# Retention stage of a two-block transformer forward: one weight split moved ahead of a wait, half splits moved into the last head, and a statistics matmul moved into the output projection

## The reference, cut to what matters

```python
def _odd_mixer(x, pos, w_in, w_out):
    p = x @ w_in                                  # 1024 -> 6144
    q, k, v, g = jnp.split(p, [qk, 2 * qk, 2 * qk + RET_MIX], axis=-1)
    q = _rope(q.reshape(B, T, RET_HEADS, RET_QK_DIM), pos)
    k = _rope(k.reshape(B, T, RET_HEADS, RET_QK_DIM), pos) * (RET_QK_DIM ** -0.5)
    ...
    # retention: (q k^T * decay) v, in chunks with a carried state
    ...
    o = of * lax.rsqrt(jnp.mean(jnp.square(of), axis=-1, keepdims=True) + EPS)
    y = o.transpose(0, 2, 1, 3).reshape(B, T, RET_MIX)
    return (jax.nn.silu(g) * y) @ w_out           # 2048 -> 1024
```

## Time and profile before

| what | value |
|---|---|
| median of three runs | 3351.13 us |
| the profiled execution's own time | 3334.76 us |
| its span in the profile | 3332.9 us |
| TensorE busy, share of the span | 2965.2 us, 89% |
| DVE, ACT, POOL busy | 1449.0, 896.7, 625.8 us |
| mean granted TensorE clock | 0.935 of full speed |
| retention, first head's start to the layer norm's end | about 734 to 1235 us of the span |
| the two expert stages | about 1795 to 2335 and 2745 to 3290 us |

### The profile page before, as it was taken

How to read it: one execution, slowest core, us unless ns; L and a number is a source line. 1 busy time by engine, 2 the same in 40 slices (tenths; PEclk the granted TensorE clock), 3 DMA queues, 4 the chain that set the end, 5 groups by cost and what they waited for, 6 DMA issues and landing times.

```text
span 3332.9 us, 42752 instructions
## 1 busy us (share of the span) xinstructions
PE 2965.2 (89%) x17700; PEld 2311.2 (69%) x17700; DVE 1449.0 (43%) x2553; ACT 896.7 (27%) x1600; POOL 625.8 (19%) x540
## 2 busy tenths in 40 slices
PE   7889999999999899999997998888598897988883
PEld 6658999998888678888786555555476675555552
DVE  4553422343444443233544443332697735533334
ACT  3442422332222334232322111111235621211111
POOL 1202201130111122011101432221200002522221
PEclk9987999999999999999998999999799998999996
DMA  4011232222221123323224999999421019999995
GB/s 133 14 63 44 71 100 85 96 73 81 80 65 66 51 76 101 101 89 101 76 76 181 374 409 409 409 408 390 156 74 59 27 36 371 406 409 410 409 409 219
DMA packets 271813, 600.30 MB, mean 180 GB/s; under 512 B 32375, under 2 KB 177202, under 8 KB 255226
## 3 DMA queue, kind: packets, MB, share of 16 engines
q1 hardware_dynamic: 247408, 569.47, 45.6%
q0 software_dynamic: 23968, 27.93, 2.6%
q10 hardware_dynamic: 234, 0.06, 0.0%
HBM read 607.75 MB, written 39.89 MB: 194 GB/s over the span
## 4 chain that ended last, share of the span: by engine, by line
PE 82%; DVE 8%; issue 4%; DMA 3%; ACT 2%; POOL 1%; SPq 1%; DVEq 0%; POOLq 0%; ACTq 0%
PE ps L101 76%; PE ps L104 6%; DVE sb_arena L126 1%; DVE sb_arena L118 1%; POOL sb_arena L118 1%; DVE sb_tmpA L118 1%; SPq L144 1%; DMA sb_ring<-in_exp_w_dram 1%; DMA sb_hx<-in_exp_w_dram 1%; DVE sb_tmpA L122 1%; DVE sb_tmpA L126 1%; DVE sb_hs L118 0%; DMA sb_arena<-x_rows,sb_smallu 0%; ACT sb_hs L112 0%; DVE sb_small L1539 0%
## 5 line engine op out<-in xcount | busy, mean ns | idle before, releaser
L101 PE MATMUL ps<-sb_hs,sb_ws 128*128 128x264 f32 (+1 forms) x6384 | 1121.1, 338 | 40.5 <-DVE sb_ws L118 27.0
L101 PEld LDWEIGHTS ps<-sb_hs,sb_ws 128*128 128x128 f32 x6384 | 985.4, 193 | 173.0 <-DVE sb_ws L118 28.1
L118 DVE TENSOR_TENSOR sb_ws<-sb_ring,sb_ws 128x1024 fp32r<-128x1024 f32 x279 | 367.4, 1320 | 431.4 <-ACT sb_ws L112 430.9
L101 PE MATMUL ps<-sb_arena 128*64 128x256 f32 (+16 forms) x2068 | 385.8, 436 | 52.9 <-issue 31.2
L112 ACT CAST sb_ws<-sb_ring 128x1024 fp32r<-128x1024 f32 x279 | 290.5, 1045 | 374.0 <-PE ps L101 356.1
L101 PE MATMUL ps<-sb_br,sb_ws 128*128 128x264 f32 (+1 forms) x2304 | 366.5, 321 | 0.0
L101 PE MATMUL ps<-sb_ring,sb_arena 128*64 128x256 f32 (+2 forms) x2314 | 319.7, 432 | 52.1 <-issue 50.9
L101 PEld LDWEIGHTS ps<-sb_br,sb_ws 128*128 128x128 f32 x2304 | 332.3, 188 | 33.7
L101 PEld LDWEIGHTS ps<-sb_arena 128*64 128x64 f32 (+6 forms) x2068 | 227.8, 167 | 156.5 <-issue 85.5
L104 PEld LDWEIGHTS ps<-sb_cst,sb_arena 128*128 128x128 f32 (+3 forms) x1032 | 155.1, 204 | 201.3 <-DVE sb_arena L118 82.2
L101 PEld LDWEIGHTS ps<-sb_ring,sb_arena 128*64 128x64 f32 (+1 forms) x2314 | 193.4, 147 | 145.6 <-issue 85.1
(11 more groups left out here) (182 smaller groups left out, 2233.6 us busy)
## 6 DMA issues: line engine op xcount, KB each, us to landing
sb_ring<-in_exp_w_dram SPq DMA_DIRECT2D x160, 1024.0 KB, 21.2
sb_hx<-in_exp_w_dram SPq DMA_DIRECT2D x128, 1024.0 KB, 21.4
sb_arena<-in_exp_w_dram SPq DMA_DIRECT2D x96, 1024.0 KB, 21.4
sb_ring<-in_mlp_w_dram SPq DMA_DIRECT2D x64, 1024.0 KB, 5.3
sb_ring<-in_od_w_in_dram SPq DMA_DIRECT2D x24, 1024.0 KB, 5.2
sb_ring<-in_conv_w_in_dram SPq DMA_DIRECT2D x12, 1024.0 KB, 5.0
sb_ring<-in_attn_w_in_dram SPq DMA_DIRECT2D x10, 1024.0 KB, 5.9
sb_ring<-in_od_w_out_dram SPq DMA_DIRECT2D x8, 1024.0 KB, 5.1
```

The source lines that it names most:

```text
L101: return self.e.matmul(o, l, r, start=start, stop=stop, skip_group_check=True)
L118: return self.e.tensor_tensor(o, a, b, op)
```

## The change

On ACT and DVE the split beside v0 (that is v2's) is now called before the wait for y0 to y3, and in the loop over v and g the first tile calls none. On ACT the upper halves of `YR` tiles 0 to 7 are made in head 3 after the copies of v, before the copies of the weighting's outputs; on DVE the lower halves follow the scores of head 3. Tiles 8 to 11 (head 2's) are split between the squares and the square root, 12 to 15 after it. On TensorE the ones matmul of head 3 is no longer ahead of the output projection but in its first pair, at step k == 4.

```diff
-        def dense(e, stage, cols, K, rhs, T, units, pair=True):
+        def dense(e, stage, cols, K, rhs, T, units, pair=True, between=None):
...
                         for k in range(kn + 2):
+                            if k == 4 and between is not None:
+                                between()
                             if k < kn:
...
-            ret_norm_pe(e, units, 3)
-            dense_all(e, ("out", 1), C4, 16, mix1_x, T2, units)
+            dense_all(e, ("out", 1), C4, 16, mix1_x, T2, units, True, lambda: ret_norm_pe(e, units, 3))
...
         def ret_act(e):
+            def late_hi(ks):
+                for k in ks:
+                    e.wait_ge(*pool_rot["y", k // 4, k % 4])
+                    e.acp(late(mix1_of(k, 0)), late(YR[:, k, :])).then_inc(*x_hi.mark(("mix1", k)))
...
+                split_hi(e)
                 if h > 0:
                     for f in range(4):
                         e.wait_ge(*pool_rot["y", h - 1, f])
-                for m in tiles(vg_cols(h)):
-                    split_hi(e)
+                for n, m in enumerate(tiles(vg_cols(h))):
+                    if n > 0:
+                        split_hi(e)
...
+                if h == 3:
+                    late_hi(range(8))
                 for f in range(4):
                     e.wait_ge(*weighed["ret", h, f])
...
             ret_squares_act(e, 3)
-            for k in range(8):
...
+            late_hi(range(8, 12))
             ret_scaled_act(e, 3)
-            for k in range(8, 16):
...
+            late_hi(range(12, 16))
...
         def ret_dve(e):
+            def late_lo(ks):
...
+                split_lo(e)
                 if h > 0:
                     for f in range(4):
                         e.wait_ge(*pool_rot["y", h - 1, f])
...
-                for m in tiles(vg_cols(h)):
-                    split_lo(e)
+                for n, m in enumerate(tiles(vg_cols(h))):
+                    if n > 0:
+                        split_lo(e)
...
+            late_lo(range(8))
             ret_squares_dve(e, 3)
...
+            late_lo(range(8, 12))
             ret_scaled_dve(e, 3)
...
+            late_lo(range(12, 16))
```

More of the change, by code:

```diff
@@ L1290, in ret_pe, with mix1_of @@
                     t.then_inc(*weighed.mark(("ret", h, f)))
-            ret_norm_pe(e, units, 3)
-            dense_all(e, ("out", 1), C4, 16, mix1_x, T2, units)
+            dense_all(e, ("out", 1), C4, 16, mix1_x, T2, units, True, lambda: ret_norm_pe(e, units, 3))
             ln_pe(e, units, 2)
+        def mix1_of(k, half):
+            return (HS, YS)[k // 8][:, half, k % 8, :]
         def mix1_x(k):
-            H_ = (HS, YS)[k // 8]
-            return late(H_[:, 0, k % 8, :]), late(H_[:, 1, k % 8, :]), x_hi["mix1", k], x_lo["mix1", k]
+            return late(mix1_of(k, 0)), late(mix1_of(k, 1)), x_hi["mix1", k], x_lo["mix1", k]
         def ret_squares_act(e, h):
@@ L1340, in ret_act @@
             ret_squares_act(e, 3)
-            for k in range(8):
-                e.wait_ge(*weighed["ret", 3, 3])
-                e.wait_ge(*pool_rot["y", k // 4, k % 4])
-                e.acp(late(HS[:, 0, k, :]), late(YR[:, k, :])).then_inc(*x_hi.mark(("mix1", k)))
+            late_hi(range(8, 12))
             ret_scaled_act(e, 3)
-            for k in range(8, 16):
-                e.wait_ge(*pool_rot["y", k // 4, k % 4])
-                e.acp(late(YS[:, 0, k - 8, :]), late(YR[:, k, :])).then_inc(*x_hi.mark(("mix1", k)))
+            late_hi(range(12, 16))
             for m in range(8):
@@ L1368, in ret_dve @@
         def ret_dve(e):
+            def late_lo(ks):
+                for k in ks:
+                    e.wait_ge(*x_hi["mix1", k])
+                    e.tt(late(mix1_of(k, 1)), late(YR[:, k, :]), late(mix1_of(k, 0)).bitcast(F), ALU.subtract).then_inc(
+                        *x_lo.mark(("mix1", k)))
             for h in range(4):
```

## The result

The kernel after took 3321.92 us (median of five runs, 3308.36 to 3323.44), the kernel before 3350.51 us in the five runs beside it (3341.43 to 3353.56): ratio 0.993, 95% interval 0.9905 to 0.9954, so 15 to 32 us faster. The two medians lie 28.6 us apart, and a ratio of 0.993 is 23.5 us.

What follows compares the result with a forecast made beforehand. Retention was taken as bound by TensorE, whose idle time was nearly all four waits for DVE's weight splits, 24.4 us. Gains of 19.5 us in the heads and 4.6 us in the tail gave 3351.13 - 24.1 = 3327.0 us, range 3322.5 to 3337.

Steps and rivals of the forecast that it cites:

- The stalls in front of v2: Heads 1 to 3: splitting v2 ahead of the wait removes stalls and slow-clock surplus, gaining 19.5 us in all.
- What is late next: Heads 1 to 3: a new stall in front of v3, between 0.5 and 1.7 us, taken as 1.7.
- Head 0: Moved split also goes ahead of rope in head 0; v3's split still ready 3.2 us early, cost nothing.
- edit 2: Halves of heads 0 and 1 made in head 3, in idle time of ACT and DVE; cost nothing.
- Edit 3: Ones matmul amid the output projection: nothing lost to speak of, but it does not set the tail.
- the tail: Behind head 3: part 2's chain over ACT and DVE ends 4.6 us earlier; bounds 2.1 and 5 us.
- Rival A: Clock falls behind the new stalls; in all three heads 17.0 us gained, 3334.1 us. Chance 0.25 (one to three heads).
- B: Turns do not hold and the split fits DVE's gap: 27.8 us gained, 3323.3 us. Chance 0.08.
- C: The tail gives half, lower halves and POOL holding each other up: 3329.3 us. Chance 0.06.
- D: Gain does not reach the end, waited away at the expert stages' weight stream: 3351 us. Chance 0.05.
- E: Slower: earlier start brings the expert weight stream into a slower regime; 3364 us at 396 GB/s. Chance 0.04.
- The carry from one execution to the median: Profiled execution's gain carried to the median of the runs: 3351.13 - 24.1 = 3327.0 us.

Runs made afterwards that it cites:

- Edit 1 alone: Only v2's split moved ahead of the wait for y0 to y3 on ACT and DVE, on the kernel before; distance 331.21 us, 19.6 us less than before.
- edit 3 alone: Only the ones matmul moved into the output projection, on the kernel before; distance 352.40 us, 1.6 us slower than before.
- without it: The change with the ones matmul put back ahead of the output projection, all else kept; distance 326.30 us, 0.3 us less than the change.
- part 2 early: The change, with part 2 of the output projection split in head 3 on ACT and DVE; distance 319.27 us, 7.35 us less than the change.
- edits 2 and 3 alone: The change with v2's split put back behind the wait for y0 to y3; distance 346.73 us, 4.1 us gained on the kernel before.
- both further edits: The change plus v3's split amid rope and part 2's split in head 3; distance 314.16 us, median 3303.64 us, ratio 0.9898 to the kernel before.

## Why the prediction was right, and where it was off

- **The stalls in front of v2 as the thing to win, with their surplus by the clock:** right. Forecast per head 5.71, 6.65 and 7.18 us; measured 5.76, 6.71 and 7.21 us. Edit 1 alone brings it. That the forecast met each head to 0.06 us is partly luck: the new stall was 0.3 us shorter than forecast (1.44 us in place of 1.7), and v3 and the gates behind it 0.28 us longer, which the sum had not foreseen; the two cancel.
- **What is late next: v3, by 1.7 us.** The right tile, the size a little off: 1.44 us. The step was the new start of rope, which I put a full microsecond later. The split does wait for y3, but saves the latency of the wait behind it, so that rope began only 0.78 us later. The kernel with the split behind the wait measured the bounds apart: turns 1.79 us, as against 2.6 us by overlap. That DVE and POOL take turns here is shown by 2.32 us for the split beside y3 and 1.23 us without, while y3 takes 2.29 us either way. The Trainium skill, page "SBUF — State Buffer", section "SBUF: two separate sides", states that of the two the one that comes second is blocked for the whole instruction of the first; these durations agree with it.
- **Head 0 and edit 2 at no cost:** right; head 0's distance from first matmul to scores is 73.58 us after, 73.80 before, and the moved halves fell into idle time: with them made, ACT was still idle for 4.62 us ahead of the first output copy, and DVE for 8.12 us ahead of the sum of squares.
- **Edit 3 worth nothing, the tail set by part 2's chain, 4.6 us:** right, 4.57 us, shown from both sides by the kernels with edit 3 alone and without it. The ones matmul stood 0.60 us for the squares, the pair ended 9.41 us ahead of part 2 ("some 10 us").
- **Rival A, the clock falls all the same:** did not happen in the change, but was nearer than it looked: at 0.35 us more it happened once in three, at 1.5 us more in three of three. Its price was put too high: the prediction gave back all of the 7.12 us for three heads, a surplus seen behind stalls of 5.9 us, and behind stalls of 1.8 to 2.9 us a fall cost 1.3 to 1.6 us.
- **Rivals B and C:** excluded. B needed a stall of 0.5 us at v3 and there were 1.44; C needed half of the tail's 4.6 us and there were 4.57.
- **Rivals D and E:** the part of the profile behind the projection's part 4 took 2173.8 us before (3332.9 - 1159.08) and 2171.5 us after (3321.6 - 1150.08). The gain reached the end.
- **The carry from one execution to the median: the one step without a ground.** "The median of the runs lies 16.4 us above the profiled one, which no edit touches; I carry the gain over." The 16.4 us are not a constant of the kernel: after the change the profiled execution lay 1.5 us above the median (3323.44 against 3321.92). The profile gained 24.2 us as forecast, and the medians lie 28.6 us apart. The 4.4 us between are no finding, as the interval of the runs goes from 15 to 32 us; but a range whose lower end allowed one microsecond for the median left them no room. That the median came out at the range's edge says nothing on the mechanism.

## What to carry to other kernels

Moving a matmul into an idle gap wins nothing where the next stall is set by a chain on other engines; what counts is which instructions stand in those engines' queues ahead of the one that TensorE waits for, and taking four upper and four lower halves out of the way (edit 2) or one split (part 2 early) was worth 4.6 and 7.4 us. Idle time that an engine has because it waits for another is not free for work that takes turns with that other one: the split put into DVE's wait for y3 won 0.35 us. A stall of TensorE costs its length and, where the clock falls, the slow stretch behind it, so taking 13.3 us of stalls away (17.6 less 4.3) won 19.7 us. And two single profiled executions are compared stage by stage from a landmark just ahead of the change, not by their spans.

## What the runs showed of the hardware

Among the twelve profiles most of the spread arises in one place. In the chain of the twelve profiles the piece of 444 matmuls that follows the first layer's attention starts anywhere from 275.96 to 298.72 us, though the piece ahead of attention starts within 136.40 to 139.47 us in all of them, and the code up to there and through attention is the same in all. Two smaller spreads come on top, of 4 us each: from there to head 0's scores it takes 524.3 to 525.6 us in seven profiles and 528.4 to 528.6 us in five (there the piece of 3132 matmuls took 390.5 us in place of 387.5 wherever the chain shows it whole), and behind part 4 2170.6 to 2174.5 us. Busy times of nearly the same 480 matmuls, first in the kernel with edits 2 and 3 alone:

```profile
170.00:298.00 128.00, 117.81 (x479) 79.58 (x478) 51.78 (x208) 41.93 (x133) 0.00 (x0) 0.56 0.10 33
```

then in the kernel with both further edits:

```profile
170.00:276.00 106.00, 90.40 (x481) 60.24 (x479) 52.88 (x208) 42.53 (x133) 0.00 (x0) 0.79 0.13 40
```

The work is equal, the granted clock 0.56 in one and 0.79 in the other. TensorE is idle for 8% of that stage in the slow one and 15% in the fast one, in gaps of up to 1.4 us; what tips the clock one way or the other there was not tried. That the same stage makes the spread among the runs of one kernel was not shown, only that it is large enough: 22.8 us there, 22.85 us among the eleven runs of the kernel before. Of these the shortest had the highest mean granted clock (0.941 at 3327.77 us) and the longest the lowest (0.929 at 3350.62 us).
